# First block of a two-block transformer: values ahead of u, V normed beside them, rotary swap by transfers

## The reference, cut to what matters

```
def _mixer(x, layer, ...):
    z = x @ w_in                                   # 256x1024 @ 1024x7168
    u, v, q, k, val, gates = split(z)
    u, v = gelu(u), gelu(v)
    v = layernorm(v)                               # over its 1024 columns
    s = einsum('gtr,bnrgc->bntgc', tril(w_s), v)   # spatial product, 8 groups, 2 chunks of 128 rows
    h_a = u * (s + b_s)
    q, k = rope(q), rope(k)                        # x1*cos - x2*sin, x2*cos + x1*sin
    o = diff_attention(q, k, val)                  # 8 heads, two maps of 64 dims each
    h_b = rmsnorm(o)
    m = g0 * (h_a @ w_branch[0]) + g1 * (h_b @ w_branch[1])
    return m @ w_out
```

## Time and profile before

| | us |
|---|---|
| runs | 1823.33, 1823.72, 1816.3 |
| median | 1823.33 |
| the profiled execution, its own time | 1826.43 |
| its span, first to last instruction | 1824.7 |
| TensorE matmul busy | 1789.1 (98%) |
| VectorE, ScalarE, GpSimd busy | 1136.3, 866.2, 249.4 |
| mean busy share of the DMA engines, by queue | 53.0% (SyncE's), 2.1% (GpSimd's) |

### The profile page before, as it was taken

One profiled execution on the slowest core, in us unless ns is written; L12 is line 12 of the kernel. 1 busy time (PEld: TensorE's weight loads), 2 busy tenths in 40 slices (PEclk: granted clock), 3 DMA queues, 4 the chain that ended last, 5 costly groups with the idle time before them and its releaser, 6 DMA issues.

```text
span 1824.7 us, 31051 instructions
## 1 busy us (share of the span) xinstructions
PE 1789.1 (98%) x12824; PEld 1618.3 (89%) x12824; DVE 1136.3 (62%) x1735; ACT 866.2 (47%) x1412; POOL 249.4 (14%) x264
## 2 busy tenths in 40 slices
PE   9999999999999999999999999999999899999998
PEld 8998699999899879997899997999787777889998
DVE  5764686686666466656675776566645555655553
ACT  5453344664445435443435753545345345445443
POOL 2000232121200020002321212000111343100000
PEclk9999999999999999999999999999999999999999
DMA  8565654446566666755745455675553333355553
GB/s 289 188 229 191 227 185 162 162 139 198 195 205 211 208 205 227 238 186 173 260 150 182 140 185 196 222 234 184 172 171 91 95 90 107 116 172 181 188 188 105
DMA packets 252397, 330.58 MB, mean 181 GB/s; under 512 B 13162, under 2 KB 213072, under 8 KB 252256
## 3 DMA queue, kind: packets, MB, share of 16 engines
q1 hardware_dynamic: 248240, 315.31, 53.0%
q0 software_dynamic: 4016, 13.27, 2.1%
HBM read 327.51 MB, written 1.05 MB: 180 GB/s over the span
## 4 chain that ended last, share of the span: by engine, by line
PE 62%; issue 24%; DVE 6%; POOL 3%; ACT 2%; DMA 2%; SPq 0%; POOLq 0%; DVEq 0%; ACTq 0%
PE bank L716 14%; PE bank L719 14%; PE bank L717 14%; PE bank L739 4%; PE bank L741 4%; PE bank L742 4%; DVE X L1939 1%; DMA G<-in_lam_dram 1%; DVE wlo L1861 1%; PE bank L1278 1%; ACT whi L1408 1%; POOL rs L2459 1%; PE bank L1256 1%; PE bank L904 1%; PE bank L942 1%
## 5 line engine op out<-in xcount | busy, mean ns | idle before, releaser
L1861 DVE TENSOR_TENSOR wlo<-raw,whi 128x1024 fp32r<-128x1024 f32 x537 | 664.2, 1241 | 383.6 <-ACT whi L1408 379.7
L1408 ACT ACTIVATE whi<-raw 128x1024 fp32r<-128x1024 f32 x549 | 574.2, 1051 | 390.5 <-PE bank L742 166.1
L716 PE MATMUL bank<-XTh,whi 128*128 128x256 f32 x1984 | 559.9, 282 | 0.0
L719 PE MATMUL bank<-XTh,wlo 128*128 128x256 f32 x1984 | 551.1, 278 | 0.0
L717 PE MATMUL bank<-XTl,whi 128*128 128x256 f32 x1984 | 550.8, 278 | 0.0
L716 PEld LDWEIGHTS bank<-XTh,whi 128*128 128x128 f32 x1984 | 373.4, 188 | 2.9
L717 PEld LDWEIGHTS bank<-XTl,whi 128*128 128x128 f32 x1984 | 374.0, 189 | 1.0
L719 PEld LDWEIGHTS bank<-XTh,wlo 128*128 128x128 f32 x1984 | 372.8, 188 | 0.4 <-DVE wlo L1861 0.3
L716 PE MATMUL bank<-HCh,whi 128*128 128x256 f32 (+1 forms) x880 | 252.4, 287 | 0.6 <-DVE tmp L2355 0.6
L717 PE MATMUL bank<-HCl,whi 128*128 128x256 f32 (+1 forms) x880 | 248.3, 282 | 0.0
L719 PE MATMUL bank<-HCh,wlo 128*128 128x256 f32 (+1 forms) x880 | 248.2, 282 | 0.0
(11 more groups left out here) (344 smaller groups left out, 2425.7 us busy)
## 6 DMA issues: line engine op xcount, KB each, us to landing
raw<-in_ffn_w_dram SPq DMA_DIRECT2D x131, 1024.0 KB, 5.1
raw<-in_w_in_dram SPq DMA_DIRECT2D x76, 1024.0 KB, 5.0
raw<-in_w_mod_dram SPq DMA_DIRECT2D x24, 1024.0 KB, 5.1
raw<-in_w_branch_dram SPq DMA_DIRECT2D x16, 1024.0 KB, 4.9
raw<-in_w_out_dram SPq DMA_DIRECT2D x12, 1024.0 KB, 4.8
raw<-in_w_ffn_gate_dram SPq DMA_DIRECT2D x11, 1024.0 KB, 5.2
raw<-in_w_ffn_up_dram SPq DMA_DIRECT2D x11, 1024.0 KB, 5.1
raw<-in_w_ffn_down_dram SPq DMA_DIRECT2D x8, 1024.0 KB, 5.2
```

Of the source, the lines that this page charges most:

```text
L716: e.matmul(o, hi[:, k, w0:w0 + nc_], xh, start=first and k == 0, stop=False)
L719: m = e.matmul(o, lo[:, k, w0:w0 + nc_], xh, start=False, stop=last and k == nk - 1)
L1408: e.activation(hi_part(n), raw_part(n), ACTF.Copy).then_inc(WHI.did(n), 1)
L1861: e.tensor_tensor(lo_part(n), raw_part(n), hi_part(n).bitcast(F32), ALU.subtract).then_inc(WLO.did(n), 1)
```

## The change

For each of the two layers of the first block:

1. The order of the weights becomes V, q and k, values, u (it was V, q and k, u, values), on every engine.
2. The swap of rotary leaves TensorE. Four transfers of 32 partitions x 1 KB each, from `mtmp` s to `mtmp` u: two issued by SyncE, behind the weight chunk that is four chunks ahead, two by GpSimd. VectorE multiplies the landed copy by sin (`times_sin`), by cos (`times_cos`) and adds (`add_parts`), which GpSimd did. `mtmp` has 8 buffers in place of 4. The permutation matrix leaves the constants.
3. Statistics and norm of V stand between the splits of the value parts.
4. The four groups of spatial matmuls stand after the blocks 1 to 4 of u.
5. A `settle` stands ahead of q and k and ahead of u; and `mod_columns` ends with one.

```diff
-        for c in range(0, 1024, 256):
-            chunk_a(w, 0, 8, c)
         for k in range(0, 8, 2):
             chunk_b(w, k, 2, 4096, 1024, MOVES)
+        for c in range(0, 1024, 256):
+            chunk_a(w, 0, 8, c)
...
+            def turned(l, n):                       # SyncE
+                ring_free(q, tm[l], ("u", n))
+                q.wait_ge(AMX, ("qk", l, n))
+                for p in (0, 32):
+                    e.dma_start(mtmp[tm[l].slot["u", n]][p:p + 32, :], mtmp[tm[l].slot["s", n]][p ^ 32:(p ^ 32) + 32, :]).then_inc(
+                        ROT[n % 4].did(("turned", l, n), by=16), 16)
...
             for c in range(1, before_bias):
                 load(c)
+                for l in range(2):
+                    if first_qk[l] <= c - 4 < first_qk[l] + 8:
+                        for j in range(2):
+                            turned(l, 2 * (c - 4 - first_qk[l]) + j)
...
                 for j in range(4):                  # mod_columns, TensorE
-                    mm = e.matmul(bank[b][:, 2 * j:2 * j + 2], spare[0:m, j * 128:(j + 1) * 128], cmb[0:m, :], start=True, stop=True)
-                mm.then_inc(MOD.did(("columns", g)), 1)
+                    e.matmul(bank[b][:, 2 * j:2 * j + 2], spare[0:m, j * 128:(j + 1) * 128], cmb[0:m, :], start=True, stop=True)
+                settle(b).then_inc(MOD.did(("columns", g)), 1)
...
-                def rotate(n):                      # mixer, TensorE
-                    b = 4 + n % 2
-                    q.wait_ge(AMX, ("qk", l, n))
-                    empty(b)
-                    e.matmul(bank[b][:, 0:T], perm, mtmp[tm[l].slot["s", n]][:, :], start=True, stop=True).then_inc(
-                        SMALL.did(("perm", l, n)), 1)
-                    emptied[b] = ((DMX, ("sin", l, n)),)
-
+                empty(3)
+                settle(3)
                 for n in range(16):
                     b = n % 4
                     empty(b)
                     gemm_a(bank[b][:, 0:T], xt, ("qk", l, n))
                     emptied[b] = ((AMX, ("qk", l, n)),)
-                    if n:
-                        rotate(n - 1)
-                for g2 in range(4):
+                gemm_b(("val", l), 8, 1, xt_b, (0, 1), [[4, 5], [6, 7]], 1024, tail=2)
+                for b in range(4, 8):
+                    emptied[b] = ((AMX, ("val", l, (b - 4) // 2, b % 2)),)
+                empty(3)
+                settle(3)
+
+                def spatial(g2):
...
                 for n in range(8):
                     b = n % 4
                     empty(b)
                     gemm_a(bank[b][:, 0:T], xt, ("u", l, n))
                     emptied[b] = ((AMX, ("u", l, n)),)
-                    if n == 0:
-                        rotate(15)
-                gemm_b(("val", l), 8, 1, xt_b, (0, 1), [[4, 5], [6, 7]], 1024, tail=2)
-                for b in range(4, 8):
-                    emptied[b] = ((AMX, ("val", l, (b - 4) // 2, b % 2)),)
+                    if 1 <= n <= 4:
+                        spatial(n - 1)
...
                 for n in range(16):                 # mixer, VectorE
                     w.pass_by(1)
+                    if n > 1:
+                        times_sin(n - 2)
                     if n:
-                        rotate(n - 1)
+                        times_cos(n - 1)
+                    if n > 1:
+                        add_parts(n - 2)
...
+                def between_val():
+                    i = calls[0]
+                    calls[0] += 1
+                    if i < 2:
+                        times_sin(14 + i)
+                        if i == 0:
+                            times_cos(15)
+                        add_parts(14 + i)
+                    if i in (2, 4):
+                        stats_v(i // 2 - 1)
+                    if i in (3, 5):
+                        norm_v(i // 2 - 1)
+                w.pass_b(8, 2, between_val)
...
+                def turned(n):                      # mixer, GpSimd
+                    ring_free(q, tm[l], ("u", n))
+                    q.wait_ge(AMX, ("qk", l, n))
+                    for p in (64, 96):
+                        e.dma_start(mtmp[tm[l].slot["u", n]][p:p + 32, :], mtmp[tm[l].slot["s", n]][p ^ 32:(p ^ 32) + 32, :]).then_inc(
+                            ROTP[n % 4].did(("turned", l, n), by=16), 16)
+
+                for n in range(16):
+                    w.pass_by(1)
+                    turned(n)
```

More of the change, by code:

```diff
@@ L197, in plan @@
 def plan(I):
-    chunks, on_dve = [], {}
+    chunks, on_dve, first_qk = [], {}, []
     def chunk_a(w, k0, nk, c0, width=256, bw=128):
@@ L236, in plan @@
             chunk_b(w, k, 2, 1024, 1024, MOVES)
+        first_qk.append(len(chunks))
         for c in range(2048, 4096, 256):
-            chunk_a(w, 0, 8, c)
-        for c in range(0, 1024, 256):
             chunk_a(w, 0, 8, c)
@@ L278, in plan @@
     parts = [(c, j) for c in range(len(chunks)) for j in range(len(chunks[c][3]))]
-    return chunks, parts, whole, on_dve, before_bias
+    return chunks, parts, whole, on_dve, before_bias, first_qk
 MOVES, STANDS = 48, 0
@@ L381, in program @@
     with ctx:
-        chunks, parts, whole, on_dve, before_bias = plan(I)
+        chunks, parts, whole, on_dve, before_bias, first_qk = plan(I)
         of_chunk = {}
@@ L395, in program @@
         BIAS = [signal(f"s_bias{h}") for h in range(8)]
+        ROT = [signal(f"s_rotary{i}") for i in range(4)]
+        ROTP = [signal(f"s_rotary_pool{i}") for i in range(4)]
         MM, TURN, SMALL, MOD = [signal("s_pe_" + n) for n in ("gemm", "turn", "small", "mod")]
@@ L1481, in mixer @@
                     q.wait_ge(MM, ("V", l, t))
-                    if t:
-                        w.more(1)
                     for c in range(2):
@@ L1511, in mixer @@
                             AMX.did(("val", l, t, c)), 1)
+                for n in range(8):
+                    w.pass_by(1)
+                    q.wait_ge(MM, ("u", l, n))
+                    ring_free(q, tm[l], ("g", n))
+                    e.activation(mtmp[tm[l].slot["g", n]][:, :], bank[n % 4][:, 0:T], ACTF.Gelu).then_inc(AMX.did(("u", l, n)), 1)
+                    if n > 1:
+                        high("ha", HAh, n - 2, mtmp[tm[l].slot["g", n - 2]], ("a", l, n - 2))
+                for n in (6, 7):
+                    high("ha", HAh, n, mtmp[tm[l].slot["g", n]], ("a", l, n))
                 q.wait_ge(DMX, ("lam", l, 1))
@@ L1951, in mixer, with stats_v @@
                 w.more(3)
-                for t in range(2):
-                    if t:
-                        w.more(1)
+                def stats_v(t):
                     for c in range(2):
@@ new lines, in mixer @@
+                calls = [0]
+                def between_val():
[11 more added lines that the diff above has]
+                w.pass_b(8, 2, between_val)
@@ L1982, in mixer, with spatial @@
+                w.more(3)
                 q.wait_ge(MIN[l], "in")
-                for g in range(8):
+                def spatial(g):
                     o = bank[6 + g // 2 % 2][:, (g % 2) * 256:(g % 2) * 256 + 256].rearrange("p (t c) -> p t c", t=2)
@@ L1994, in mixer @@
                     w.pass_by(1)
-                    if n == 0:
-                        rotate(15)
-                    else:
-                        low("ha", HAl, HAh, n - 1, mtmp[tm[l].slot["g", n - 1]])
-                low("ha", HAl, HAh, 7, mtmp[tm[l].slot["g", 7]])
-                w.pass_b(8, 2)
-                w.more(3)
+                    if 1 <= n <= 4:
+                        spatial(2 * n - 2)
+                        spatial(2 * n - 1)
+                    if n > 1:
+                        low("ha", HAl, HAh, n - 2, mtmp[tm[l].slot["g", n - 2]])
+                for n in (6, 7):
+                    low("ha", HAl, HAh, n, mtmp[tm[l].slot["g", n]])
                 for j in range(2):
```

70 lines of the change are left out of this document (30 added, 40 removed).

## The result

The changed kernel takes **1802.55 us** (median of 4 runs, 1801.19 to 1805.51) against 1822.38 for the kernel before on the same chip (4 runs, 1816.3 to 1823.72): ratio 0.990, interval 0.9874 to 0.9926. That is 20 us faster where 28 were forecast (13 to 23 by the interval); the prediction had 1797 with a range of 1789 to 1811. The profiled execution took 1801.19 us, its span 1799.4; the one before 1826.43.

A forecast was written before the change was run, and what follows sets the result against it. TensorE's instruction stream was taken as the bound. Gains of 17.9, 1.4 and 8.9 us less 0.3, with gates 0.1 faster each layer, made 28 us: from 1826.43 to 1798.4, taken as 1797; range 1789 to 1811.

The forecast's parts named there:

- no product stretch at 0.118: Sign that the forecast is right: no 128x256 products of q, k, u or feed-forward step at 0.118 us.
- q and k 43.6: Sign that the forecast is right: q and k last 43.6 us from the transpose to the values.
- feed-forwards still at 511: Sign that transposes don't set the pace: feed-forward windows still hold 511 matmuls in 60 us.
- the pace theory: 128x256 products run at 0.1133 us instead of 0.1178 behind a lone settle transpose, so added settles make them faster.
- q and k, 8.95 per layer: Mixer's q and k: 52.58 us become 43.6 without rotary matmuls and wait, at the fast pace; 17.9 us in all.
- u and spatial, 0.7 per layer: Mixer's u with spatial groups between its blocks: 26.81 us become 26.1; 1.4 us in all.
- Feed-forwards, 8.9 us: Settles ending `mod_columns` put two slow feed-forward stretches, 768 and 1188 products, at 0.1133: 3.5 and 5.4 us saved.
- The first rival: Transposes don't set the pace, so no pace gain comes: 1809 us; chance 0.13.
- V's norm: V's statistics and norm, 9.2 us on VectorE, move to the value splits: 0; lead gone, 1.0 us per layer returns.
- The swap's latency: Rotary's transfers in q and k cost 0, as TensorE waits only if they land over 11.2 us after a block.
- X: Time from a block's end on TensorE until both queues' swap transfers have landed; 1.6 to 9 us, taken as 7.
- Its threshold of 1.36 per issue: In q and k, two GpSimd issues per block set the block's length from 1.36 us each; GpSimd rival's chance 0.04.

The follow-up runs named there:

- the second profile: The changed kernel once more, nothing edited, in its second profiled execution; median 1804.49 us, ratio 0.9902.
- One load later: Changed kernel with SyncE's half of the swap issued one load (two blocks) later, GpSimd's half as it was; 1871.19 us, ratio 1.0272.
- the kernel with eight: Changed kernel with GpSimd's half of the swap cut into eight transfers a block instead of two, same bytes; 1835.51 us, ratio 1.0079.
- the fourteen executions: One profiled execution each of the kernel before, the changed kernel and the twelve experiments, which include the changed kernel once more.

## Why the prediction held, and which terms did not

The time was 5.5 us above the forecast and inside the range, even inside the narrower 1792 to 1804. The second is in part luck: the mixers' 15.9 us off the median of before, 1822.38, give 1806.5, and the same kernel came to 1804.49 when it was run again. Of the signs named ahead, "no product stretch at 0.118" and "q and k 43.6" failed at once; "feed-forwards still at 511" didn't show, so the signs alone would have left the pace theory standing. By its terms:

- **q and k, 8.95 per layer: 7.27 came** (52.58 to 45.31). The step "384 x 0.1133" was mis-sized: the pace behind the settle was 0.118. The rest of the term is right: a rotary matmul costs 0.41 measured by putting it back (0.44 at one pace), 0.43 forecast, and the wait of 1.0 per layer went. In layer 1 of the second profile, where the fast pace came, the stage took 43.63, to the digit what was forecast.
- **u and spatial, 0.7 per layer: 0.69 came**, by two errors that cancel. Three quarters of the products, 144, ran at 0.118 instead of 0.1133 (144 x 0.0045 = 0.65 more). And a group costs 3.62 (304.18 to 307.80) less 24 x 0.1133, or 0.90, instead of 1.05 (0.6 less for four).
- **Feed-forwards, 8.9 us: the step that failed**, together with the sentence that behind a settle the pace is "always" 0.113. The profiled execution did show it, 4.0 and 5.3 us. But the settle alone in the kernel before is worth 1.5 us, by its interval between 3 lost and 6 gained, and taking it out of the changed kernel changes nothing that the runs can tell. The profiled execution of before had the slow pace in its longest stretch and in one of its two stretches of 768 products, and a tally over one execution took that for a law. The prediction had the clue: "runs take different paces behind `mod_columns`, I think", and a slow stretch behind four transposes, put down as an exception. That stretch was no exception, since there the pace changed every time. And "24 of 24 elsewhere" had missed one: in the same trace the 24 products from 1474.72 stand behind the transposes of L1203, and step by 0.118.
- **The first rival** (transposes don't set the pace, 1809) was right that a settle brings no fast pace, and had 0.13. The medians lie between it and the forecast. The mixers' 15.9 us lie inside the interval of the measured gain, 13 to 23, so the 4 us beyond them in the medians aren't told from scatter.
- **The rule with one fixed addition per matmul** (the Trainium skill, "TensorE: Matmul & The Clock Gate", section "Wait — 56ns, not 53.3ns?") doesn't describe this stream: 257 and 268 matmuls in 30 us, one program, one execution. Its consequence, that a settle buys nothing, agrees with the measured medians within their intervals, but for another reason.
- **V's norm: 0 for its move held; its price if the lead were gone did not.** "Its 1.0 us per layer would come back" should have been 4 to 5 us per layer. I priced the work alone, not that the first transfers would start behind it.
- **The swap's latency, term 0, held; the room up to 11.2 us did not.** A transfer lands 4.3 us (SyncE) or 3.9 us (GpSimd) after its issue, both medians, and X, read for each of the 32 blocks of the changed kernel, was 3.4 to 7.3 us, where 7 was taken. (The split that stands behind the transfers of block n is that of part n+6, not n+5; it is wanted five blocks after block n's end, as the sum has it.) But the formula "5 x 2.72 - 2.4" let SyncE issue when it liked. Its issues are tied to the loads, and the loads to the splits. One load later the kernel lost 67 us, and X was no constant: in layer 0 SyncE's half landed 11.4, 16.0, 22.0 and 26.6 us after the ends of blocks 0, 2, 4 and 6, each lap later than the last until TensorE was held to the same pace. The sentence "SyncE's next load waits behind the transfers, ... about as late: 0" saw the tie and priced it at its best case.
- **GpSimd.** The row of before (0.58 per issue) was the right witness, and the fivefold growth of the Trainium skill, "SBUF — State Buffer", section "SBUF: two separate sides", did not show: all 64 issues of the changed kernel took 0.498 to 0.543, and the 256 of the kernel with eight 0.496 to 0.541, beside a VectorE at work. The prediction had left out the rule's condition. The section names VectorE operations in a two-port performance mode, and those with two inputs in SBUF only against a GpSimd operation that itself reads SBUF. In which mode VectorE's operations ran, no run shows. The traces agree with the second: GpSimd's additions, which read SBUF, took 1.65 beside a split and 0.73 alone, while its issues stayed at 0.5 and landed after 3.9 us (median). What the prediction said of issues too slow for the block was borne out at the one point tried: with eight issues, at 4.0 us per block, the kernel stands at 1.0079, slower than before. Its threshold of 1.36 per issue wasn't tried.

## What to carry to other kernels

Work that TensorE does only to move data can go to DMA queues and give back its whole price (here 0.41 to 0.44 us a matmul), if the consumer takes it up two blocks later and nothing in either queue's order can make the transfer wait for the work that waits for it. Before pricing such a transfer by its latency, write down the ring of queue, buffer and split that it closes, and look at what one step later would do. And before a difference in pace is made a term, compare two executions of one program: what differs between equal stages of one execution, or between two executions, can't be counted on as a gain.

## What the runs showed of the hardware that was not expected

- Two paces of the same 128x256 products, 0.1133 and 0.1178 us, both at a granted clock of 1.00. Where TensorE doesn't wait, a pace holds through a stretch of 384 to 1188 products, but for the first few. No settle, and no number of them, fixed it. Directly behind a 128x512 product it was slow in 40 of 40 places; behind a group of spatial products in u, and behind the four transposes in the last feed-forward, it changed in 130 of 130.
- A second difference of this kind in the layernorm ahead of the mixer, where VectorE's pass over X runs beside GpSimd's splits. The kernel before and the changed one, VectorE's and GpSimd's timelines:

```profile
193.21 4.79 POOL L2425 TENSOR_TENSOR wlo<-raw,whi 128x1024 fp32r<-128x1024 f32 x2
193.26 5.83 DVE L1939 SCALAR_TENSOR_TENSOR X<-X,rs,gb 128x1024 f32<-128x1024 f32 x1 [0.48 <-POOL rs L2459]
```

```profile
195.05 5.69 POOL L2463 TENSOR_TENSOR wlo<-raw,whi 128x1024 fp32r<-128x1024 f32 x2
195.10 3.41 DVE L1946 SCALAR_TENSOR_TENSOR X<-X,rs,gb 128x1024 f32<-128x1024 f32 x1 [0.48 <-POOL rs L2497]
```

The pass over the other row tile, with no split beside it, takes 1.28. It looks as if VectorE's pass waited for both of GpSimd's splits in the first kernel, and came between them in the second, where the two splits take 0.9 longer; no run tests this. Over the fourteen executions it took 5.8 in 13 of 28 places ahead of a mixer and 3.4 in the others, in the second profile of the changed kernel 3.44 ahead of the first mixer and 5.79 ahead of the second. It's worth 2.4 us of TensorE's time each (its waits for this pass are 6.3 and 3.9 us in all in the two kernels), and part of why single executions differ by several us.
- GpSimd's issue of a transfer within SBUF takes 0.498 us beside a VectorE that is busy, less than the 0.58 of its broadcast load; while its additions beside a split had doubled.
